# The norms' sums of squares in two short-format matmuls in place of one float32 matmul

## The reference

```
xn   = rmsnorm(x, norm1_g)
proj = xn @ w_in                      # x_a | x_b | g_a | g_b
y_a  = rg_lru(causal_conv4(x_a))      # two gates by block matmuls, then a scan in time
y_b  = (window means of x_b - x_b) @ pool_w * pool_scale
x    = x + (sigmoid(g_a)*(y_a @ w_br_a) + sigmoid(g_b)*(y_b @ w_br_b)) @ w_out
x    = x + (silu(g)*u) @ w_down,  g|u = rmsnorm(x, norm2_g) @ w_gu    # D_FF = 2816
y    = rmsnorm(x, final_g)

rmsnorm(x, g) = x * rsqrt(mean(x*x, axis=-1) + 1e-6) * g
```

## Time and profile before

| | |
|---|---|
| median of 3 runs | 2940.25 us (2940.04 to 2941.14) |
| profiled execution | 2941.63 us |
| its span | 2939.8 us |
| TensorE matmul busy | 2874.5 us, 98% |
| VectorE busy | 1956.4 us, 67% |
| ScalarE busy | 1263.1 us, 43% |
| DMA | 354.43 MB, mean 121 GB/s |

### The profile page before, as it was taken

How to read it: one execution, slowest core, us unless ns; L and a number is a source line. 1 busy time by engine, 2 the same in 40 slices (tenths; PEclk the granted TensorE clock), 3 DMA queues, 4 the chain that set the end, 5 groups by cost and what they waited for, 6 DMA issues and landing times.

```text
span 2939.8 us, 37519 instructions
## 1 busy us (share of the span) xinstructions
PE 2874.5 (98%) x15006; PEld 2829.8 (96%) x15006; DVE 1956.4 (67%) x2946; ACT 1263.1 (43%) x1745; POOL 0.2 (0%) x4
## 2 busy tenths in 40 slices
PE   8799999999999999999999999999999999999998
PEld 7789999999999999999999999999999999999998
DVE  7657666667576676776666757766667576666656
ACT  4743433347434333483333325833333366343222
POOL 0000000000000000000000000000000000000000
PEclk9999999999999999999999999999999999999999
DMA  4263333333334333333333333334333333333332
GB/s 142 83 219 110 137 122 115 115 108 124 130 118 142 115 108 122 107 117 130 129 130 109 122 115 117 129 115 138 115 115 117 120 110 122 111 107 127 115 117 81
DMA packets 113163, 354.43 MB, mean 121 GB/s; under 512 B 12128, under 2 KB 30816, under 8 KB 112992
## 3 DMA queue, kind: packets, MB, share of 16 engines
q1 hardware_dynamic: 102480, 336.14, 33.2%
q10 hardware_dynamic: 10512, 15.90, 1.6%
HBM read 339.12 MB, written 12.87 MB: 120 GB/s over the span
## 4 chain that ended last, share of the span: by engine, by line
PE 84%; DVE 9%; ACT 3%; issue 2%; DMA 1%; SPq 0%; ACTq 0%; DVEq 0%
PE ps L294 84%; DVE gb L705 2%; DVE wring L827 2%; DVE main L713 1%; DVE ylo L710 1%; DVE tot L660 1%; ACT wring L407 1%; DVE tmp L739 1%; ACT L489 0%; DVE rstd_n L666 0%; DMA fused<-main 0%; PE ps L313 0%; ACT tmp L489 0%; ACT tmp L480 0%; ACT tmp L482 0%
## 5 line engine op out<-in xcount | busy, mean ns | idle before, releaser
L294 PE MATMUL ps<-yhi,wring 128*128 128x416 f32 x4800 | 1312.3, 352 | 1.1 <-DVE wring L827 1.1
L827 DVE TENSOR_TENSOR wring<-wraw,wring 128x1024 fp32r<-128x1024 f32 x610 | 746.2, 1224 | 328.4 <-ACT wring L407 327.0
L294 PE MATMUL ps<-xhi,wring 128*128 128x416 f32 (+1 forms) x3200 | 890.7, 357 | 41.6 <-DVE wring L827 40.3
L294 PEld LDWEIGHTS ps<-yhi,wring 128*128 128x128 f32 x4800 | 900.7, 188 | 10.6 <-issue 1.8
L294 PE MATMUL ps<-ylo,wring 128*128 128x416 f32 x2400 | 841.1, 350 | 0.0
L407 ACT ACTIVATE wring<-wraw 128x1024 fp32r<-128x1024 f32 x610 | 640.9, 1051 | 459.3 <-PE ps L294 438.0
L294 PEld LDWEIGHTS ps<-xhi,wring 128*128 128x128 f32 x3200 | 610.5, 191 | 54.7 <-DVE wring L827 37.7
L294 PE MATMUL ps<-xlo,wring 128*128 128x416 f32 (+1 forms) x1600 | 568.4, 355 | 0.0
L294 PE MATMUL ps<-hhi,wring 128*128 128x416 f32 x1760 | 485.0, 352 | 0.0
L294 PEld LDWEIGHTS ps<-ylo,wring 128*128 128x128 f32 x2400 | 452.2, 188 | 5.1 <-issue 1.4
L294 PEld LDWEIGHTS ps<-hhi,wring 128*128 128x128 f32 x1760 | 329.3, 188 | 2.4
(11 more groups left out here) (108 smaller groups left out, 1520.5 us busy)
## 6 DMA issues: line engine op xcount, KB each, us to landing
wraw<-dwm SPq DMA_DIRECT2D x577, 512.0 KB, 3.2
wraw<-fused SPq DMA_DIRECT2D x40, 512.0 KB, 3.2
dy<-main ACTq DMA_DIRECT2D x36, 208.0 KB, 2.1
xres<-dx ACTq DMA_DIRECT2D x32, 208.0 KB, 3.0
sraw<-dws SPq DMA_DIRECT2D x24, 256.0 KB, 3.8
fused<-main SPq DMA_DIRECT2D x16, 256.0 KB, 7.0
xres<-dx SPq DMA_DIRECT2D x4, 216.0 KB, 5.7
xres<-dx ACTq DMA_DIRECT2D x4, 216.0 KB, 6.0
```

What stands on the lines that cost most here:

```text
L294: mm = nc.tensor.matmul(out, wt[:, c * P:(c + 1) * P], x, start=(first and q == 0), stop=(last and q == 2))
L827: V.tensor_tensor(wring[:, n % RING, 1, :], wraw[:, n % RAW, :], wring[:, n % RING, 0, :].bitcast(f32), SUB).then_inc(w_lo, 1)
```

## The change

`column_sum` waits for two new semaphores in place of `sq_summed`, and issues two matmuls with the same ones (now of the short format) on a high and a low part of `tot`. ScalarE makes the high part (`sum_part`: a copy that rounds), VectorE the low part (`sum_rest`: `tot` minus the high part). The parts lie in buffers that are free at the time: tile 7 of yhi/ylo for the first n1, tile 7 of xhi/xlo for the later ones, tile 0 of hhi/hlo for n2 and n3.

```diff
-        ones = sb("ones", [P, P])
+        ones = sb("ones", [P, P], f32r)
...
+        sum_hi, sum_lo = sem("sum_hi"), sem("sum_lo")
...
+        def sum_parts(kind, b):
+            if kind == "n1":
+                hi, lo = (xhi, xlo) if b else (yhi, ylo)
+                return hi[:, 7, 0:BW[b]], lo[:, 7, 0:BW[b]]
+            return hhi[:, 0, :], hlo[:, 0, :]
+
+        def sum_index(kind, b):
+            return sq_index(kind, b, 0) // 8
...
             def column_sum(name, kind, b):
-                pe.wait_ge(sq_summed, sq_index(kind, b, 7) + 1)
+                pe.wait_ge(sum_hi, sum_index(kind, b) + 1)
+                pe.wait_ge(sum_lo, sum_index(kind, b) + 1)
                 free(name)
                 width = BW[b] if kind == "n1" else LW
-                nc.tensor.matmul(bank(name)[:, 0:width], ones[:], tot[:, 0:width], start=True, stop=True).then_inc(ready, 1)
+                hi, lo = sum_parts(kind, b)
+                nc.tensor.matmul(bank(name)[:, 0:width], ones[:], hi, start=True, stop=False)
+                nc.tensor.matmul(bank(name)[:, 0:width], ones[:], lo, start=False, stop=True).then_inc(ready, 1)
...
+            def sum_part(kind, b):
+                act.wait_ge(sq_summed, sq_index(kind, b, 7) + 1)
+                A(sum_parts(kind, b)[0], tot[:, 0:BW[b] if kind == "n1" else LW], ACT.Copy).then_inc(sum_hi, 1)
...
+            def sum_rest(kind, b):
+                hi, lo = sum_parts(kind, b)
+                dve.wait_ge(sum_hi, sum_index(kind, b) + 1)
+                V.tensor_tensor(lo, tot[:, 0:BW[b] if kind == "n1" else LW], hi.bitcast(f32), SUB).then_inc(sum_lo, 1)
```

More of the change, by code:

```diff
@@ L549, in _ @@
                     split_hi(2)
+            sum_part("n1", 0)
             split_side(0)
@@ L619, in _ @@
                         load_x(b + 1, m)
+                sum_part("n2", b)
                 ahead(b, "g", 0)
@@ L632, in _ @@
                             square("n1", b + 1, k, xres[:, k, 0:BW[b + 1]])
+                        sum_part("n1", b + 1)
                     if i == 4 and not last:
@@ L640, in _ @@
                     square("n3", b, m, main[:, m, :])
+                sum_part("n3", b)
             root(("n3", NB - 1, 0), 2)
@@ L838, in _ @@
             V.memset(epsc[:], EPS)
-            V.memset(ones[:], 1.0).then_inc(setup, 1)
+            V.memset(ones[:].bitcast(f32), 1.0).then_inc(setup, 1)
             dve.wait_ge(consts_in, 16)
@@ L860, in _ @@
                     split_lo(2)
+            sum_rest("n1", 0)
             split_side(0)
@@ L960, in _ @@
                     square_sum("n2", b, m)
+                sum_rest("n2", b)
                 ahead(b, "g", 0)
@@ L972, in _ @@
                         square_sum("n3", b, 7)
+                        sum_rest("n3", b)
                     elif i:
@@ L978, in _ @@
                             square_sum("n1", b + 1, k)
+                        sum_rest("n1", b + 1)
                     if i == 4 and not last:
```

## The result

Over 20 runs each, the kernel with the change takes 2944.66 us (2943.0 to 2946.46) and the kernel before 2940.97 (2939.48 to 2944.21): a ratio of 1.0012, 95% interval 1.0006 to 1.0017, so 3.7 us slower: within the 0.2% that counts as no change, though the interval of the ratio lies above 1. The forecast was 2944.5, 4.2 us slower than the 2940.25 it started from. The profiled execution took 2944.49 us with a span of 2942.7, 2.9 longer than before's.

The account below looks back on a forecast made before the run. TensorE (98% busy) was taken to bound the kernel, except at block boundaries, where VectorE and ScalarE hold the chain. Terms -2.9 + 4.8 + 1.2 + 0.4 + 0.7 = +4.2 us gave 2944.5 us, range 2940.5 to 2948.4.

Parts of the forecast that it names:

- The saving: Inside blocks, nine n2 and n1 sums on TensorE each give up 0.32 us: -2.9 us.
- The handshake at the boundaries: At four boundaries, ScalarE's copy and VectorE's subtraction for n3 lengthen TensorE's wait by 1.20 us each: +4.8 us.
- VectorE is full for 38 us: Behind n3's last addition VectorE is busy 37.2 of 38.1 us, so added work reaches TensorE's wait in full.
- The cover at n2 and n1: Inside blocks, VectorE's idle time covers the 1.2 us copy and subtraction: cost 0, against 11 us without cover.
- The start: At the first n1, copy and subtraction make the reciprocal and first evictions 1.2 us later: +1.2 us, bound 0.
- The end: At the last n3, copy, subtraction and two short matmuls replace two float32 passes of 1.73 us: +0.4 us.
- the pair of matmuls at half speed: In the last column sum, two short matmuls were taken to last 0.92 us with TensorE at half speed.
- The table load: Before the last root, a 1.28 us load stays hidden; rival with a drain behind it: +1.1 us, chance 0.03.
- The clock: Behind longer boundary waits TensorE's granted clock falls: +0.7 us together; rival with further slow stretches: 2948.5 us, chance 0.20.
- a rival: At boundaries, something like a ScalarE store issue takes up the copy's part, leaving 0.5 us each: 2940.5 us, chance 0.13.

Follow-up runs that it names:

- e5: Kernel before, with the plain float32 sum of n2 and of n1 of blocks 1 to 4 issued twice: 2946.21 against 2941.51 us, ratio 1.0016.
- e3: The whole change, with VectorE's n3 subtraction at the four boundaries moved behind the next block's first weight split: 2942.35 us against the change's 2944.66.
- e1: The change for n2 and n1 of blocks 1 to 4 only; n3 and first n1 keep plain float32 sums: 2938.71 us against 2940.96 for the kernel before.
- e6: The whole change, but TensorE waits for the low part only ahead of the second matmul: 2943.66 us in a single run.
- e10: Kernel before, with two short matmuls for the nine inner sums and the four stores issued behind the third group of gates: 2937.20 against 2941.16 us.
- e2: The change for n3 and the first n1 only; the nine inner sums stay plain: 2948.23 us against 2940.96 for the kernel before, ratio 1.0024.
- e4: The whole change, with n3's copy and subtraction made twice in turn at the four boundaries: 2950.45 us, 5.8 slower than the change.
- e7: Kernel before, with ScalarE's four stores of y moved from ahead of the first group of gates to behind it: 2939.65 against 2941.51 us.

## Why the prediction was right

The forecast of 2944.5 lies 0.16 us from the median. That is closer than its terms were: it started from a median of 2940.25 that 20 runs put at 2940.97, 0.7 higher, and its step of 4.2 was 0.5 too long. The mechanism, a saving inside the blocks and a larger cost at the boundaries, is shown.

**The saving.** -2.9 us on nine inner sums: shown. Each gives up 0.32 us (0.70 to 0.38 in the trace), and with those alone the kernel is 2.3 us faster at the median, and in its trace the last sum starts 2.60 earlier (2925.08 for 2927.68). The other side of the same term, nine more float32 sums in e5, counted at 0.70 each as far as the trace can be read free of the stores.

**The handshake at the boundaries.** +4.8 us: shown, 1.20 at the third boundary by the rows, and by its dose (1.21, 1.26, 1.24, 1.15 for one more). The step behind it, that VectorE is full for 38 us and so passes on what is put in front, is what made the forecast; a share of 67% over the whole span does not show it. That 0.7 of the 1.20 is VectorE waiting for ScalarE is shown by e3.

**The cover at n2 and n1.** Cost 0: shown by e1, which has all nine of them and no new wait at a sum.

**The start.** +1.2 forecast. The reciprocal that follows the first n1 starts 1.17 us later (24.22 before):

```profile
25.39 2.85 DVE L695 RECIPROCAL rstd_n<-rstd_n 128x432 f32<-128x432 f32 x1
```

It stands at 23.90 to 24.32 in every trace with the plain first sum and at 25.18 to 25.45 in every one with the parts. What of it leaves block 0 is less sure: the first wait behind the mixer ends at 200.54 to 201.59 without the change at the start and at 201.48 to 203.86 with it (e6 and e10 show none), so the 1.29 of the pair compared above is one draw from a spread of over 1 us. No run has the change at the start alone.

**The end.** +0.4 forecast, +0.57 in the trace (1.80 to 2.37). The mis-sized term is the pair of matmuls at half speed: 0.92 us came from two in the middle of a stream; from a standstill the pair took 1.05 (0.68, then 0.36 behind it). That half speed was met at all is not fixed: before's last float32 sum took 1.73 us, at a clock of 0.50, but the same sum took 0.96 and 0.97 in e1 and e5, at 1.00. The 0.57 compares two executions that both met the low clock. The table load was hidden, as the row had it: in the trace of the change it stands from 2930.51 to 2931.79, and the root starts at 2932.29, when TensorE is done. By the 2.66 us that the Trainium skill gives for a switch of table set ("ScalarE: Activation LUTs", section "What ACT_TABLE_LOAD costs"), the root could not have started before 2933.17, an estimate; the trace disagrees by 0.88 us.

**The clock.** +0.7 forecast, nothing measured beyond 0.1, and here a step of the prediction was wrong: it took 7 x (1 - share) as time lost, less the small waits behind. The first boundary lost 1.8 us of clock, as priced, where I had left 0.4 of it as cost; all of it vanished. The same held before the change. e5's third boundary is at 1.00 over 16 us and takes 222.80 us to the reciprocal behind n2's sum, 222.10 without its extra 0.70; before's, at 0.89, takes 222.05. So in these stretches a slower TensorE cost nothing, and the waits for VectorE's splits behind most boundaries point to VectorE as what sets the pace. With that the terms are -2.9 + 4.8 + 1.3 + 0.6 = +3.8, beside the 3.7 measured; the stores are left out of it.

**What the prediction didn't see.** The four store issues on ScalarE differ by up to 1.4 us between the traces (1.95 in e5 to 3.40 in e1), on the chain. I had put such an issue only in a rival, as something that could take up part of the handshake. It made the profiled difference 2.9 instead of 3.8, and the third wait 4.19 us where 5.0 was forecast; at the second (6.04 for 6.4) some 0.3 of the delay stands just ahead of the wait. What makes an issue longer was not settled, nor whether it goes with the execution or with the kernel: each kernel has one trace. At the third boundary it took 2.85, 2.91 and 2.43 us before and in e1 and e3, and 1.96 to 1.98 in the change, e2, e4, e5 and e6. If that 0.87 belongs to the change, the sum is 2.9, and 0.8 of the 3.7 has no term, so the agreement of 3.8 with 3.7 is in part luck.

## What to carry to other kernels

Before a matmul is made cheaper by giving other engines more to do, look at each of its places apart: the same 0.32 us was worth having in nine places and was lost in six, where the helper engines were the chain. Here a handshake between two engines cost an engine with a backlog the sum of both operations, 1.20 us, and 0.7 of it went when the second half was put one instruction later. A store issue that was moved within a stretch where it was on the chain came back as another wait. A fallen clock is priced by what the next mark on the chain loses, and not by the share alone: here that was nothing.

## What the runs showed of the hardware

Four store issues of 208 KB each on ScalarE's queue held it for 1.95 (e5) to 3.40 us (e1) in the same place of nearly the same program, and for 1.84 us in e7 behind the first group. A float32 sum of 416 columns took 0.70 us on the chain, two float32r matmuls in its place 0.38. The granted clock over 16 us around a wait of 5.4 to 6.0 us was 0.79 in every case of e4, no lower than around one of 3.87 us before; behind waits of 4.17 and 4.18 us it was 0.89 and 0.79. The last float32 sum took 0.96 and 0.97 us at a clock of 1.00 (e1, e5) and 1.73 at 0.50 (before).
